# Moving the shift of the second layer's modulation, and the root behind its RMSNorm, onto ScalarE in a two-layer hybrid encoder step

## The reference

```python
def rmsnorm(x, g):
    y = xf * lax.rsqrt(jnp.mean(xf * xf, axis=-1, keepdims=True) + EPS)
    return (y * g)
...
    h = rmsnorm(x, g) * (1 + scale[:, None]) + shift[:, None]
...
    u = jnp.dot(h, w_in)
```

## Time and profile before

| | us |
|---|---|
| median of 3 runs | 2416.9 |
| the runs | 2414.41, 2418.08, 2416.9 |
| the profiled execution, its own time | 2413.58 |
| its span, first to last instruction | 2411.8 |
| PE busy | 2318.1 (96%) |
| DVE, ACT, POOL busy | 975.1, 817.7, 819.4 |
| mean granted clock of PE | 0.981 of full |

### The profile page before, as it was taken

The page is one execution under the profiler, slowest core; times in us unless marked ns, Lnnn a source line. Parts: engine busy times, 40 slices in busy tenths (PEclk is TensorE's granted clock), DMA queues, the critical chain, the costliest instruction groups (busy, mean ns, idle before and its releaser), DMA issues.

```text
span 2411.8 us, 47057 instructions
## 1 busy us (share of the span) xinstructions
PE 2318.1 (96%) x18307; PEld 2160.3 (90%) x18307; DVE 975.1 (40%) x1898; ACT 817.7 (34%) x1560; POOL 819.4 (34%) x620
## 2 busy tenths in 40 slices
PE   7799999999999999989987999999999999999997
PEld 4478899999999998989986889999999999998997
DVE  4454466563111223451128446776411123344113
ACT  2233343343333333342223333445333333343221
POOL 0232233333333332344424323343433333344441
PEclk9799999999999999999998999999999999999999
DMA  8975566664333332224423553333333333223443
GB/s 292 376 252 172 165 188 193 211 208 120 89 92 90 84 83 77 76 85 148 125 88 88 176 162 102 79 84 84 102 89 92 90 84 79 71 82 107 132 132 128
DMA packets 442882, 312.15 MB, mean 129 GB/s; under 512 B 21304, under 2 KB 413376, under 8 KB 441480
## 3 DMA queue, kind: packets, MB, share of 16 engines
q1 hardware_dynamic: 414480, 283.17, 40.2%
q10 hardware_dynamic: 28216, 26.39, 3.6%
HBM read 280.81 MB, written 30.92 MB: 129 GB/s over the span
## 4 chain that ended last, share of the span: by engine, by line
PE 91%; DVE 3%; DMA 3%; DVEq 1%; issue 0%; ACTq 0%; ACT 0%; SPq 0%
PE proj L641 24%; PE proj L647 24%; PE proj L643 24%; DMA work<-in_w_ada 3%; PE proj L710 2%; PE misc L911 2%; PE misc L756 2%; PE misc L884 2%; PE proj L741 2%; PE misc L835 1%; PE misc L893 1%; PE misc L594 1%; PE proj L693 1%; PE proj L694 1%; PE proj L697 1%; PE proj L721 1%
## 5 line engine op out<-in xcount | busy, mean ns | idle before, releaser
L641 PE MATMUL proj<-act_hi,w_hi 128*128 128x288 f32 x4288 | 1212.9, 298 | 0.0
L517 POOL TENSOR_TENSOR w_lo<-raw,w_hi 128x512 fp32r<-128x512 f32 x560 | 739.8, 1323 | 1363.0 <-ACT w_hi L1108 1314.4
L643 PE MATMUL proj<-act_lo,w_hi 128*128 128x288 f32 x4288 | 1194.7, 294 | 0.0
L647 PE MATMUL proj<-act_hi,w_lo 128*128 128x288 f32 x4288 | 915.9, 295 | 0.0
L641 PEld LDWEIGHTS proj<-act_hi,w_hi 128*128 128x128 f32 x4288 | 805.7, 188 | 22.2 <-issue 19.2
L643 PEld LDWEIGHTS proj<-act_lo,w_hi 128*128 128x128 f32 x4288 | 806.3, 188 | 2.3
L647 PEld LDWEIGHTS proj<-act_hi,w_lo 128*128 128x128 f32 x4288 | 686.3, 188 | 0.0
L1108 ACT ACTIVATE w_hi<-raw 128x512 fp32r<-128x512 f32 x536 | 337.6, 631 | 1017.8 <-PE proj L647 1006.5
L1475 DVE SCALAR_TENSOR_TENSOR xy<-misc,hg,xy 128x512 f32<-128x512 f32 (+1 forms) x32 | 16.5, 517 | 228.0 <-PE misc L911 228.0
L1475 DVE SCALAR_TENSOR_TENSOR acc<-work,kw_tok,acc 128x256 f32<-128x256 f32 (+3 forms) x128 | 90.2, 726 | 39.1 <-ACT work L1190 30.4
L1475 DVE SCALAR_TENSOR_TENSOR xy<-proj,mod,lb 128x288 f32 (+5 forms) x66 | 23.5, 411 | 178.7 <-PE proj L647 172.1
(11 more groups left out here) (230 smaller groups left out, 2315.8 us busy)
## 6 DMA issues: line engine op xcount, KB each, us to landing
raw<-in_w_in SPq DMA_DIRECT2D x448, 256.0 KB, 2.9
xy<-in_w_ada SPq DMA_DIRECT2D x64, 1024.0 KB, 7.9
work<-in_w_ada SPq DMA_DIRECT2D x32, 1024.0 KB, 10.4
raw<-in_w_out SPq DMA_DIRECT2D x128, 256.0 KB, 2.8
x_keep<-xy ACTq DMA_DIRECT2D x32, 288.0 KB, 2.6
lb<-x_keep SPq DMA_DIRECT2D x24, 288.0 KB, 3.3
x_keep<-xy ACTq DMA_DIRECT2D x4, 1152.0 KB, 8.1
out_y_prompt<-work SPq DMA_DIRECT2D x4, 1024.0 KB, 4.6
```

The source lines that it names most:

```text
L517: pool.tensor_tensor(w_lo[:, c, :, 0:width], raw[:, c, :, 0:width], w_hi[:, c, :, 0:width].bitcast(F32), ALU.subtract)\
L641: pe.matmul(dst, w_hi[:, c, kk, :], act_hi[:, k, cols], start=(k == 0), stop=False)
L643: pe.matmul(dst, w_hi[:, c, kk, :], act_lo[:, k, cols], start=False, stop=False)
L647: m = pe.matmul(proj[b][:, half, 0:HALF], w_lo[:, c, kk, :], act_hi[:, k, cols], start=False, stop=(k == KT - 1))
```

## The change

In both layers ACT reads the sum of squares from PSUM itself and takes the root of (sum / 2048 + eps) in one instruction; DVE then takes the reciprocal of the root (`invert_root`) and goes on without a further wait. In layer 1 alone, ACT writes the high parts of the weight chunks 0 to 3 before it waits for the sum, with a small `Sqrt` on one column behind them; and DVE no longer adds the shift: it raises `norm_x` after the two multiplications, and ACT adds the shift in place with two `Identity` activations that take it as their bias, drains, and then writes the high part as before. The low parts are made from the shifted `xy` as before. Everything else stays.

```diff
--- before.py
+++ after.py
@@ -1108,8 +1108,6 @@
                         act.activation(w_hi[:, c, :, :], raw[:, c, :, :], ACT.Copy)\
                             .then_inc(hi_ready, 1)
 
-                root(r_x, 0)
-
                 def upper_front(n):
 
                     at, w = n % RING, front_width(n)
@@ -1121,6 +1119,11 @@
 
                     for k in range(k0, k1):
                         hold(act, norm_x, l * 2 * KT + k + 1)
+                        if l > 0:
+                            for a, z, w in PARTS:
+                                act.activation(xy[:, k, a:z], xy[:, k, a:z], ACT.Identity,
+                                               bias=mod_of[l][:, k, w:w + 1])
+                            act.drain()
                         act.activation(act_hi[:, k, :], xy[:, k, :], ACT.Copy).then_inc(h_split, 1)
 
                 def take(t, b, pairs, free):
@@ -1139,12 +1142,20 @@
                     act.drain().then_inc(t_read, 1)
 
 
+                if l > 0:
+                    for n in FRONT_CHUNKS[0]:
+                        upper_front(n)
+                    act.activation(rinv[:, 0:1], eps[:, :], ACT.Sqrt)
+                hold(act, ss_made, l * 3 + 1)
+                act.activation(halves(r_x), wide(proj[0]), ACT.Sqrt, scale=1.0 / D_MODEL, bias=eps[:, :])\
+                    .then_inc(ms_ready, 1)
+
                 for c in range(5):
                     if c > 0:
                         upper_h((c - 1) * KC, c * KC)
                     if l == 0 and 0 < c < 4:
                         keep_first(c)
-                    for n in FRONT_CHUNKS[c]:
+                    for n in FRONT_CHUNKS[c] if c > 0 or l == 0 else ():
                         upper_front(n)
                     if l == 0 and c == 0:
                         decay(0)
@@ -1517,13 +1528,11 @@
                 tt(dst[:, a:z], dst[:, a:z], sq[:, a:z], ALU.add)
                 dve.drain().then_inc(sq_used, 1)
 
-            def mean_square(ps, dst, n, value):
-
-                hold(dve, ss_made, value)
-                dve.tensor_scalar(halves(dst), wide(ps), 1.0 / n, EPS, ALU.mult, ALU.add)
-                dve.drain()
-                dve.reciprocal(dst, dst)
-                dve.drain().then_inc(ms_ready, 1)
+            def invert_root(l):
+
+                hold(dve, ms_ready, l * 3 + 1)
+                dve.reciprocal(r_x, r_x)
+                dve.drain().then_inc(r_ready, 1)
 
             def read_rows(j):
 
@@ -1563,7 +1572,7 @@
                 dve.tensor_scalar(sp_[:, 4, :], p_, 2.0, None, ALU.mult)
                 dve.tensor_scalar(sp_[:, 5, :], p_, -4.0, None, ALU.mult)
 
-            mean_square(proj[0], r_x, D_MODEL, 1)
+            invert_root(0)
             read_rows(0)
             hold(dve, vec_made, 2)
             for n in range(DEPTH):
@@ -1604,9 +1613,8 @@
                         .then_inc(h_low_v, 1)
 
                 if l > 0:
-                    mean_square(proj[0], r_x, D_MODEL, l * 3 + 1)
+                    invert_root(l)
                     hold(dve, x_kept, l * KT * 16)
-                hold(dve, r_ready, l * 5 + 1)
                 if l == 0:
                     for c in range(4):
                         hold(dve, x_first[c], 16)
@@ -1630,9 +1638,6 @@
                         for a, z, w in PARTS:
                             stt(xy[:, k, a:z], xy[:, k, a:z], mod[:, KT + k, w:w + 1], r_x[:, a:z],
                                 ALU.mult, ALU.mult)
-                        dve.drain()
-                        for a, z, w in PARTS:
-                            dve.tensor_scalar(xy[:, k, a:z], xy[:, k, a:z], mod[:, k, w:w + 1], None, ALU.add)
                         dve.drain().then_inc(norm_x, 1)
                         if k % 2 and k > 1:
                             lower(k - 2, 0)
```

## The result

The changed kernel takes 2401.49 us in the median of four runs (2397.21 to 2402.64), the kernel before 2417.49 in four (2414.41 to 2419.7). The ratio is 0.9938, with a 95% interval of 0.9924 to 0.9952: 12 to 18 us gone. Against these the gain would be 13 to 14 us.) The profiled execution took 2397.21 us, with a span of 2395.4 against 2411.8. The forecast was 2400, for a gain of 15.2 in the profile.

The account below looks back on a forecast made before the run. VectorE was taken to pace layer 1's front, TensorE what follows. Gains of 7.7 us before chunk 0's end and 7.5 behind make 15.2: 2398.4 from the profiled execution, 2401.7 from the median, forecast 2400, range 2394 to 2411.

Parts of the forecast that it names:

- What bounds it: Start of layer 1: VectorE sets the pace, 52 us for 16 pieces, 18 us of them collisions with GpSimd; TensorE bounds afterwards.
- Root: Square root on ScalarE straight from PSUM: 0.77 us, 0.8 us gained in layer 1; layer 0 gains 0, bounds -0.2 and +0.2.
- the 1.2 us held against it: Allowance in layer 1 for the 3.75 us reciprocal meeting the last weight split: 0 taken, up to 1.2 us against.
- the prediction's 0.8 us: Layer 1: VectorE's first multiplication starts at 1264.7 instead of 1265.5 through the new root, bounds 0.5 and 1.0 us.
- Weights ahead: High parts of chunks 0 to 3 before layer 1's sum: cost 0, possibly 0.7 us from colliding with VectorE's addition of squares.
- Shift: Shift moved to ScalarE in layer 1: 0.96 us for two activations, drain 0.16, 1.75 us a piece, bounds 1.6 and 2.4.
- Up to X: Layer 1 until chunk 0 is used: reached at 1276.0 against 1283.7, a gain of 7.7 us.
- Behind X: Layer 1 from chunk 1 to chunk 10: waits of 3.6 and 1.2 us and half clock vanish, 7.5 us gained.
- Behind the front: After layer 1's swap: modulation weights land in 7.9 us, TensorE has some 13 us of work, so nothing is given back.
- No new table load: Sign against the rival that Identity costs two loads a piece in layer 1: 22 us late, 2438 us, chance 0.04.
- The clock did not stay low: Rival: TensorE stays at 1.2 GHz through chunks 1 and 2, 5.6 us lost, time 2404 to 2407, chance 0.08.
- The dearer step: Rival: ScalarE needs 2.4 us a piece in layer 1, gain only 5.5 us, time 2408 to 2411, chance 0.14.

Follow-up runs that it names:

- e2: The change, but with the high parts of chunks 0 to 3 behind the root on ScalarE again; median 2403.00 us, ratio 0.9951 to the kernel before.
- e7: The change plus a ScalarE copy of each piece onto itself and a drain; median 2408.20 us, ratio 0.9975 to the kernel before.

## Why the prediction was right, point by point

- **What bounds it.** Right. The shift on VectorE was the pace: alone it is 9.4 of 13.0 us, and the other two parts without it are 2.6.
- **Root.** Sized right: 0.74 us for the activation (0.77 said), the reciprocal at 0.80 us behind the sum's end, 3.75 us long and not stretched, so the 1.2 us held against it did not come (nor in `e2`, where it ran beside the splits nearly throughout); the prediction's 0.8 us is what the chunks-and-shift run lacks. In layer 0 the multiplications start at 49.65 instead of 49.88, 0.2 us, the bound that I had named.
- **Weights ahead.** Right that they cost nothing: VectorE's addition of the squares, beside the first split, took 0.76 us as before. What the prediction missed is that the root's new place brings most of this by itself. Its text treats the two as separate gains; with the shift on ScalarE the explicit order is worth 0.44 us.
- **Shift.** ScalarE's step is 1.60 us where I took 1.75; the two activations are 0.94 to 0.96 (0.96 said), but the drain costs 0.07 and not the 0.16 that I read from another place. The row that I read stands before an instruction that also waits on semaphores, and was the wrong one for a drain between two of the engine's own instructions.
- **Up to X.** X, the end of chunk 0, was to come 16.0 us after the sum's end (1276.0 less 1260.0). ScalarE's `w_hi` of chunk 4, which waits for exactly this, starts at 1273.43, 16.1 us after the sum's end at 1257.31. That the two agree so well is partly luck, for two misses cancel: the fourth quarter began 15.0 us after the sum's end (14.6 said), but the clock had returned by then, and it took 0.83 us (1272.34 to chunk 1 at 1273.17) and not 1.50.
- **Behind X, the step that failed:** "PE asks for piece 7 at X + 8.8. So the wait of 3.6 us there is just gone." It shrank to 1.08 us, and the same again at piece 11, for which the prediction had said "no wait". The term that was mis-sized is the 1.1 us from ScalarE's last piece to its low part (X + 7.7 to X + 8.8). It measured 2.5: ScalarE was done with piece 7 at 1280.49, 0.4 us better than said, and the low part was there at 1282.98. VectorE came late, since its multiplications of pieces 8 and 9 took 3.15 us beside GpSimd's low part, where the same four operations take 2.01 alone (1272.16). Then the low part itself ran 1281.25 to 1282.98, twice its length: GpSimd's split of chunk 5 had begun at 1281.08. (The Trainium skill's rule of the shared port pair, SBUF — State Buffer, "SBUF: two separate sides", cited in the prediction, fits this row too: 1.73 against 0.76 us.) The prediction counted GpSimd against VectorE up to chunk 0 but not behind it. The two orders of VectorE show it: with the multiplications moved into VectorE's idle time, both waits go, while ScalarE's step stays as it is. These 2.2 us are all that separates 15.2 from 13.0.
- **Behind the front.** Right: TensorE is busy throughout from 1308, and nothing is given back. The total reached 16 us all the same, through the 3.4 us outside the front. That the time came within 1.5 us of the forecast is thus luck in part: the front gave 2.2 us less than forecast, and a scatter outside it, which no run explains, made up for that.
- **Rivals.** No new table load: Identity ran at 0.71 us for 512 columns after Copy, Square and Sqrt, and ScalarE's load counts are those of the kernel before. This is now shown here, as the Trainium skill's page on ScalarE: Activation LUTs ("Table sets: the hidden batching unit") had it. That page's rule to put additions on VectorE (the Trainium skill, ScalarE: Activation LUTs, "Rules for kernel authors") would have cost 10 us of front here, 62.85 against 52.50: it compares one instruction with another and not the queues that they stand in. The clock did not stay low: the first matmul of a quarter takes 0.33 us at 1272.34, and chunks 1 and 2 ran at a granted 1.00 (1273 to 1279.5, busy throughout). The dearer step was made in `e7` and is answered there.

The last wait of any size is that for the first low part, 9.0 us: square, addition, sum, root, reciprocal (3.75), multiplication, shift, copy and subtraction, one behind the other.

## What to carry to other kernels

When an engine is the pace of a staged hand-over, look for what else it does per item, and count what its port partner does to it in every round, not only in the first. When work is moved ahead, check whether another move in the same change has not already freed the place: here root and weight chunks each cleared the same collision, and the second was worth 0.4 to 0.8 us. And place an engine's slack work in its idle stretches on the timeline, since multiplying four pieces costs 5.4 us alone and 9 us beside GpSimd.

## What the runs showed of the hardware that was not expected

**Waits of the same length were followed by different clocks.** In the run with the dearer step, waits of 1.52 and 0.74 us came twice. The first pair (before 1286.37 and 1288.13) left the clock at 1.00; the second (before 1298.47 and 1300.23) was followed by five microseconds at 0.66, some 1.7 us of work lost on top of 2.3 us of waiting. In the change, waits of 1.08 us at chunks 3 and 6 left it at the upper level too (0.33 us for the first matmul behind each). Between the last matmul of layer 0 and the sum lie 3.62 us of idle in the change and in the chunks-and-shift run alike; the sum ran at 0.50 in the one and at 1.00 in the other.

**The same loop at the same granted clock had different paces.** The output tiles of layer 0 are a loop that no kernel here changes, and TensorE is busy in it at 1.00 throughout. ScalarE's square marks each tile. Before:

```profile
1117.21 0.69 ACT L1064 ACTIVATE sq<-xy 128x576 f32 x1 [1.37 <-DVEq L1969]
1129.74 0.69 ACT L1064 ACTIVATE sq<-xy 128x576 f32 x1 [1.25 <-DVEq L1969]
...
1243.51 0.69 ACT L1064 ACTIVATE sq<-xy 128x576 f32 x1 [1.26 <-DVEq L1969]
```

After:

```profile
1116.24 0.69 ACT L1064 ACTIVATE sq<-xy 128x576 f32 x1 [1.36 <-DVEq L1974]
1128.60 0.69 ACT L1064 ACTIVATE sq<-xy 128x576 f32 x1 [1.25 <-DVEq L1974]
...
1240.93 0.69 ACT L1064 ACTIVATE sq<-xy 128x576 f32 x1 [1.25 <-DVEq L1974]
```

The ten tiles from the first to the last row take 126.30 us before and 124.69 after. The run with the late chunks took 12.9 us a tile in layer 0 and 12.5 in layer 1. This is the larger part of the 2.7 us ahead of the front. Its cause was not found. Nor is the start of the kernel constant: the first rotation of layer 0 came between 154.5 and 157.9 us in the profiled executions, behind the modulation weights' transfers. A difference of 2 or 3 us between two medians of this kernel is thus nothing that a small edit can claim; the stretch around the edit can.
